# Two raw slots and three slots of split weights instead of four and two, with the split at the middle of a tile

## What is computed

```python
for i in range(DEPTH):
    h = rmsnorm(x, norm_g[i])
    proj = jnp.einsum('bsd,dn->bsn', h, w_in[i])
    ...
    ya = forgetting_attention(qa, ka, va, logf) * jax.nn.silu(za)
    yb = nsa_attention(qb, qb_rot, k_cmp, v_cmp, k_sel, vsb, k_win, vwb, gates) * jax.nn.silu(zb)
    yc = differential_attention(qc, kc, vc, lam, lam_init, diff_subln_g[i]) * jax.nn.silu(zc)
    g = jax.nn.sigmoid(mg).reshape(B, S, N_BRANCH, D)
    merged = g[:, :, 0] * (ya @ w_br_a[i]) + g[:, :, 1] * (yb @ w_br_b[i]) + g[:, :, 2] * (yc @ w_br_c[i])
    x = x + merged @ w_out[i]
    x = x + jax.nn.sigmoid(x @ w_ple_gate[i]) * (p[i] @ w_ple[i])
return rmsnorm(x, final_g)
```

## Time and profile before

| | us |
| --- | --- |
| median of 3 runs | 1508.64 |
| lowest, highest | 1507.59, 1510.21 |
| the profiled execution's own time | 1507.86 |
| its span in the profile | 1506.0 |
| PE busy | 1476.4 |
| DVE busy | 939.5 |
| ACT busy | 635.4 |

### The profile page before, as it was taken

One profiled execution on the slowest core, in us unless ns is written; L12 is line 12 of the kernel. 1 busy time (PEld: TensorE's weight loads), 2 busy tenths in 40 slices (PEclk: granted clock), 3 DMA queues, 4 the chain that ended last, 5 costly groups with the idle time before them and its releaser, 6 DMA issues.

```text
span 1506.0 us, 22241 instructions
## 1 busy us (share of the span) xinstructions
PE 1476.4 (98%) x7765; PEld 1225.9 (81%) x7765; DVE 939.5 (62%) x2197; ACT 635.4 (42%) x1499; POOL 75.4 (5%) x79
## 2 busy tenths in 40 slices
PE   8999999999999999999999999999999999999997
PEld 6778888888888887887787887888888888878885
DVE  6866765655656676454576668655555666755544
ACT  6543434444444444343444434344344444434343
POOL 1000000000001000000100000000000010000011
PEclk9999999999999999999999999999999999999998
DMA  7324443324325553332332335423343354433232
GB/s 196 90 78 119 112 113 78 73 75 107 77 69 134 140 129 87 100 101 70 109 104 77 106 100 135 109 58 76 80 100 81 99 129 124 112 99 109 80 88 74
DMA packets 259262, 150.48 MB, mean 100 GB/s; under 512 B 47482, under 2 KB 247764, under 8 KB 259156
## 3 DMA queue, kind: packets, MB, share of 16 engines
q1 hardware_dynamic: 259156, 149.11, 37.9%
HBM read 118.67 MB, written 2.10 MB: 80 GB/s over the span
## 4 chain that ended last, share of the span: by engine, by line
PE 79%; DVE 8%; DMA 4%; ACT 3%; SPq 2%; issue 2%; POOL 1%; ACTq 0%; DVEq 0%
PE D L774 21%; PE D L776 20%; PE D L775 19%; PE Ob L965 7%; PE T L943 4%; DMA arena<-rcs 3%; DVE w_lo L1329 2%; PE S L930 2%; PE S L931 2%; SPq L593 1%; ACT w_hi L1095 1%; PE S L920 1%; DMA rcs<-rx 1%; SPq L675 1%; ACT probs L1207 1%
## 5 line engine op out<-in xcount | busy, mean ns | idle before, releaser
L774 PE MATMUL D<-h_hi,w_hi 128*128 128x512 f32 x1264 | 537.9, 426 | 2.7 <-DVE w_lo L1329 1.7
L776 PE MATMUL D<-h_lo,w_hi 128*128 128x512 f32 x1264 | 496.1, 392 | 0.0
L775 PE MATMUL D<-h_hi,w_lo 128*128 128x512 f32 x1264 | 494.3, 391 | 0.0
L1329 DVE TENSOR_TENSOR w_lo<-raw,w_hi 128x512 fp32r<-128x512 f32 (+2 forms) x504 | 292.9, 621 | 256.3 <-ACT w_hi L1095 255.2
L1095 ACT ACTIVATE w_hi<-raw 128x512 fp32r<-128x512 f32 (+2 forms) x504 | 263.5, 569 | 245.8 <-PE D L776 243.5
L1207 ACT ACTIVATE probs<-probs,nmax 128x128 f32<-128x128 f32 (+3 forms) x256 | 142.0, 555 | 331.6 <-DVE nmax L1580 331.5
L776 PEld LDWEIGHTS D<-h_lo,w_hi 128*128 128x128 f32 x1264 | 237.2, 188 | 53.1
L774 PEld LDWEIGHTS D<-h_hi,w_hi 128*128 128x128 f32 x1264 | 238.8, 189 | 45.7 <-issue 6.3
L775 PEld LDWEIGHTS D<-h_hi,w_lo 128*128 128x128 f32 x1264 | 239.3, 189 | 30.3 <-issue 0.5
L1580 DVE CUSTOM_DVE_ANT_0 probs<-S,maskb 128x128 f32<-128x128 f32 (+3 forms) x256 | 115.1, 487 | 25.0 <-PE S L931 12.3
L556 DVE COPY pT<-T 128x128 f32<-128x128 f32 (+3 forms) x160 | 77.6, 487 | 59.5 <-PE T L943 59.0
(11 more groups left out here) (249 smaller groups left out, 1602.4 us busy)
## 6 DMA issues: line engine op xcount, KB each, us to landing
raw<-in_w_in_dram SPq DMA_DIRECT2D x124, 512.0 KB, 3.9
arena<-rcs SPq DMA_DIRECT2D x48, 256.0 KB, 4.4
raw<-in_w_in_dram SPq DMA_DIRECT2D x32, 256.0 KB, 3.7
arena<-rcs SPq DMA_DIRECT2D x64, 128.0 KB, 2.3
raw<-in_w_out_dram SPq DMA_DIRECT2D x16, 512.0 KB, 4.0
raw<-in_w_ple_gate_dram SPq DMA_DIRECT2D x16, 512.0 KB, 4.1
rcs<-rx SPq DMA_DIRECT2D x80, 64.0 KB, 2.0
raw<-in_cmp_w_k_dram SPq DMA_DIRECT2D x8, 512.0 KB, 3.7
```

The costliest lines, as they stand in the source:

```text
L774: pe.matmul(o, w_hi[:, sl, cs], hi[:, k, :], start=(k == 0), stop=False)
L775: pe.matmul(o, w_lo[:, sl, cs], hi[:, k, :], start=False, stop=False)
L776: ins = pe.matmul(o, w_hi[:, sl, cs], lo[:, k, :], start=False, stop=last)
L1329: TT(w_lo[:, sl, half], raw[:, ring(L, t, RAW), half], f(w_hi[:, sl, half]), ALU.subtract).then_inc(M["dve_lo"], 1)
```

## The change

`raw` gets two slots instead of four and the split weights three instead of two; the memory of both together stays the same. `weight_halves` goes: ACT and DVE split both halves of tile t + 2 when they come to the step in the middle of tile t. SP loads tile t + 4 instead of t + 6 at the end of tile t, and at a layer's start two tiles ahead of the small loads, two behind them. The loops are written out, since the slot of a tile (modulo 3) isn't the same in both turns; in them ACT and DVE ask for the split of tile t + 2 at the same place as before. In the gate phase both halves come ahead of the wait for the gate.

```diff
-RAW = 4
-SPL = 2
+RAW = 2
+SPL = 3
...
-def weight_halves(tiles, t):
-
-    nxt = tiles[t + 1][0] if t + 1 < len(tiles) else None
-    if nxt in ("w1k", "w1v"):
-        return ((), (0, 1)) if tiles[t][0] == "za" else ((0,), (1,))
-    if nxt and kt(nxt) == 8 and tiles[t][0] not in ("kcb", "vcb"):
-        return (), (0, 1)
-    return (0, 1), ()
...
-                    for t in range(RAW, 6):
+                    for t in range(RAW, 4):
                         static_load(t)
...
-                        if it[0] == "end" and it[1] + 6 < T0 + 4:
-                            static_load(it[1] + 6)
+                        if it[0] == "end" and it[1] + 4 < T0 + RAW:
+                            static_load(it[1] + 4)
...
-                    with pe.Fori(0, NM // 2 - 2) as i:
+                    for i in range(NM // 2 - 2):
...
-                                dense(kind, t, k)
+                                dense(kind, t + 4 * i, k)
...
                     for it in items:
                         what = it[0]
+                        if what == "mm" and it[2] == steps(tiles[it[1]][0]) // 2:
+                            hi(it[1] + 2)
...
                             D = Dn[ring(L, t, 2)]
-                            ahead, behind = weight_halves(tiles, t)
-                            if ahead:
-                                hi(t + 2, parts=ahead)
...
-                            if behind:
-                                hi(t + 2, parts=behind)
...
                         t = T2 + 2 * m
-                        weights_ahead(t, (0,))
+                        weights_ahead(t, (0, 1))
                         act.wait_ge(M["pe_dense"], t + 1)
                         act.wait_ge(M["dve_evac"], DE2 + m - 1)
                         A(th[:, m % 2, :], Dn[ring(L, t, 2)][:], ACT.Tanh, scale=0.5).then_inc(M["act_evac"], 1)
-                        weights_ahead(t, (1,))
                         weights_ahead(t + 1, (0, 1))
...
                         elif what == "mm":
                             t, k = it[1:]
+                            if k == steps(tiles[t][0]) // 2:
+                                lo(t + 2)
                             if (t, k) == (0, NM - 1):
                                 norm_chain()
...
-                            ahead, behind = weight_halves(tiles, t)
-                            lo(t + 2, parts=ahead)
...
-                            lo(t + 2, parts=behind)
```

More of the change, by code:

```diff
@@ L1023, in _ @@
                         ins.then_inc(M["pe_p"], 1)
-                    with pe.Fori(0, NM // 4) as i:
+                    for i in range(NM // 4):
                         for j in range(4):
@@ L1033, in _ @@
                                     pe.wait_ge(M["dve_merge"], k + 1)
-                                dense("out", t, k)
+                                dense("out", t + 4 * i, k)
                     def xg_transpose(m):
@@ L1080, in _, with hi @@
                     M, raw_ld, last_layer = MM[L], raw_lds[L], L == DEPTH - 1
[L1081 to L1092, removed]
+                    def hi(t, parts=(0, 1)):
+                        sl, n = ring(L, t, SPL), kt(kind_of(t)) * P
+                        act.wait_ge(raw_ld[t % RAW], landed_at(t))
+                        if t >= SPL:
+                            act.wait_ge(M["pe_dense"], t - SPL + 1)
+                        elif L:
+                            act.wait_ge(MM[L - 1]["pe_dense"], slot_user(t, SPL) + 1)
                         for h in parts:
@@ L1237, in _ @@
                     hi(T0 + 3)
-                    with act.Fori(0, NM // 2 - 2) as i:
+                    for i in range(NM // 2 - 2):
                         for j in range(4):
                             t = T0 + 2 + j
-                            hi(t + 2, i)
+                            hi(t + 2 + 4 * i)
                             if j % 2 == 0:
@@ L1261, in _ @@
                         A(y_hi[:, c, :], b[:], ACT.Copy).then_inc(M["act_p"], 1)
-                    with act.Fori(0, NM // 4) as i:
+                    for i in range(NM // 4):
                         for j in range(4):
                             t = T1 + j
-                            hi(t + 2, i)
+                            hi(t + 2 + 4 * i)
                             act.wait_ge(M["dve_evac"], i * 4 + (DE1 + j + 1))
@@ L1322, in _, with lo @@
                     TT, STT, TS, RED = dve.tensor_tensor, dve.scalar_tensor_tensor, dve.tensor_scalar, dve.tensor_reduce
-                    def lo(t, i=None, k=8, parts=(0, 1)):
-                        sl, n = ring(L, t, SPL), (kt(kind_of(t)) if i is None else k) * P
+                    def lo(t, parts=(0, 1)):
+                        sl, n = ring(L, t, SPL), kt(kind_of(t)) * P
                         for h in parts:
                             half = slice(h * n // 2, (h + 1) * n // 2)
-                            dve.wait_ge(M["act_hi"], 2 * t + 1 + h if i is None else i * 8 + (2 * t + 1 + h))
+                            dve.wait_ge(M["act_hi"], 2 * t + 1 + h)
                             TT(w_lo[:, sl, half], raw[:, ring(L, t, RAW), half], f(w_hi[:, sl, half]), ALU.subtract).then_inc(M["dve_lo"], 1)
@@ L1677, in _ @@
                         TT(acc[:, n, :], acc[:, n, :], rt[:], ALU.add).then_inc(M["dve_acc"], 1)
-                    with dve.Fori(0, NM // 2 - 2) as i:
+                    for i in range(NM // 2 - 2):
                         for j in range(4):
                             t = T0 + 2 + j
-                            lo(t + 2, i)
+                            lo(t + 2 + 4 * i)
                             if j % 2:
@@ L1712, in _ @@
                         TT(y_lo[:, c, :], b[:], f(y_hi[:, c, :]), ALU.subtract).then_inc(M["dve_p"], 1)
-                    with dve.Fori(0, NM // 4) as i:
+                    for i in range(NM // 4):
                         for j in range(4):
```

## The result

The changed kernel takes 1527.78 us (median of four runs, 1526.98 to 1528.33) against 1509.22 us of the kernel before beside it: a ratio of 1.0124, 95% interval 1.0112 to 1.0137. It is slower by 18.6 us, where the forecast was 7.4 us and the range ended at 1524. The profiled execution has a span of 1525.8 us, 19.8 more than before.

The account below looks back on a forecast made before the run. TensorE, busy 1476.4 of 1506.0 us, was taken as the bound. Losses of 18.0 us less gains of 10.6 gave net +7.4, so 1515.3 profiled and 1516 as the median; range 1509 to 1524.

Parts of the forecast that it names:

- own signs of being wrong: PE's layer-start wait under 2 us, keys' low half not delayed, or new waits over 0.5 us in stages 4 to 7.
- The forecast's own case: Whole kernel: losses of 18.0 us less gains of 10.6, net +7.4, 1516 us; chance 0.42.
- The clock falls: Rival, start of layer 1: PE's hold of some 5 us lowers the clock, 3 us more, 1519; chance 0.27.
- Loss 4: Stages 8 to 10: splits between high and low halves delay queries' and keys' low halves; 5.7 us, bounds 0 to 9.
- Loss 1: Start of layer 1: tile 2's late load and its split hold up the norm chain and PE; 4.8 us, bounds 3 to 6.
- Loss 2: Start of layer 0: ScalarE's copies for tile 2 precede tile 0's evacuation, delaying PE; 0.9 us, bounds 0 to 1.2.
- Loss 3: Stage 3: tile 31's late load delays PE 2.9 us, 5.8 in both layers; a hold before tile 19, 0.8 in both.
- The gains: Waits removed: gate phases 3.6 us, stage 0 1.7, stages 0 to 3 2.8, unit 11 2.0, stages 4 to 7 0.5; 10.6 together.
- Two slots are enough: Rival, stages 3 and 8 to 10: loads land before ScalarE asks, so 4 us faster, 1504.6; chance 0.09.
- Holds everywhere: Rival: some thirty late loads per layer each show on PE by 0.15 us, 8 us more, 1524; chance 0.13.
- It comes out even: Rival: the losses of stages 3 and 8 to 10 come at half, about +1.5 us, 1510; chance 0.09.

Follow-up runs that it names:

- e9: Kernel before, loops written out, plus four planted TensorE holds in the output projection (6, 7, 8 and 10 VectorE sums): 1541.91 us.
- e10: Kernel before, loops written out, plus four planted TensorE holds in the output projection (4, 5, 5 and 4 VectorE sums): 1521.13 us.
- e15: Kernel before, loops written out, plus four planted TensorE holds in the output projection (5 VectorE sums each): 1524.42 us, one run.
- e2: Changed kernel, with the weights of the kc tiles and the brb tile behind zc split one step later in stages 8 to 10: 1513.0 us.
- e1: Changed kernel, with layer 1's load of tile 2 back ahead of the wait for the layer's end and the eight small loads: 1519.35 us.
- e13: Changed kernel, with layer 1's weights of tile 2 split behind the norm chain and their load left late: 1518.89 us.
- e12: Kernel before, loops written out, with two raw slots and loads two tiles later, splits at their old places: 1507.96 us.
- e7: Changed kernel with the edits of e1 and e2, and the load at each tile's end issued ahead of the swap: 1499.98 us.
- e11: Changed kernel, with splits back at the places of the kernel before and loads issued ahead of the swaps: 1513.87 us.

## Why the prediction was wrong

The direction and the places were right; the size was not, 18.6 us for 7.4. Of the prediction's own signs of being wrong none came: PE's wait at the layer's start was 5.6 us, the keys' low half was later, and no new wait of over 0.5 us stands in stages 4 to 7. Two steps failed.

**The clock had no term in the sum.** The forecast's own case left it out; the rival *The clock falls* had it, but only in the start of layer 1, at 3 us, and gave 1519. Losses 3 and 4 were forecast as holds too, the largest of 2.9 us, and the step that failed is that I asked of the longest hold alone whether it would bring the clock down. The changed kernel fell in five places: tiles 32 and 76 in two layers, 6.4 us by their shifts, and 2.7 of the 8.18 at the start of layer 1 (PE's 5.80 us from 773.20 on ran at a mean of 0.54, so 5.3 us at the lower level), 9.1 us in all. e9, e10 and e15 show that a hold alone does this. The Trainium skill's statement (TensorE: Matmul & The Clock Gate, Loop structure matters more than you think) that waits between matmuls can leave the engine at the lower clock is what the trace shows, at five places and not one; it had been right to take it as a rival and wrong to give it one place.

**Loss 4 was mis-sized**: 5.7 us forecast, 10.3 measured without the clock (2.86 + 2.97 in layer 0, 2.85 + 0.45 + 1.15 in layer 1). The delay of one low half was right, 0.66 us for the 0.7 to 1.3 said. What was missing is that I took queries and keys each by itself, while the keys' swap waits for the queries' put, so that they add, and that a later put may also take longer to land: 2.8 us at the keys' put in layer 1, for the 1.25 of the sum. e2 shows the order as the cause. In layer 0 the last part of the keys' put for unit 10 also took 6.5 us from issue to landing (510.96 to 517.44), 4.8 in layer 1. Two weight loads were issued behind it at 512.21 and 514.87, and the DMA engines were busy 0.95 of the time from 514.5 to 517.5; but layer 1 has two such loads as well, so what made the difference stays open.

**Loss 1** was right: 4.8 forecast, 8.18 less 2.7 of clock measured, 5.5. The start of layer 1 in the changed kernel (it answers to the earlier trace rows):

```profile
764.01 1.06 SPq L614 DMA_DIRECT2D raw<-in_w_in_dram  x2
...
768.47 1.15 ACT L1081 ACTIVATE w_hi<-raw 128x512 fp32r<-128x512 f32 x2 [7.22 <-DMA raw<-in_w_in_dram]
769.13 1.29 DVE L1311 TENSOR_TENSOR w_lo<-raw,w_hi 128x512 fp32r<-128x512 f32 x2 [5.32 <-ACT w_hi L1081]
...
770.34 0.16 DVE L1348 TENSOR_SCALAR nrm<-T 128x4 f32<-128x4 f32 x1
...
773.17 2.08 PE L834 MATMUL T<-rcs,ones 128*128 128x512 f32 x2 [5.61 <-DVE rcs L1354]
```

The load is issued behind the small ones, ScalarE waits for it, VectorE for ScalarE, the norm chain stands behind both, and PE behind the chain, where 2.08 us for two matmuls (1.12) shows the clock at once. e1 and e13 add that it takes both, the late load and the split ahead of the chain: mending either takes the hold and its clock away, with 0.2 us left in e1 and 1.2 in e13.

**Loss 2** was 0.9 and is 0.86. **Loss 3** was 5.8 for tile 31 and is 4.2 (2.21 + 1.98), 0.8 for tile 19 and none there, but 0.95 at tile 27. The path was the one described: the load of tile 31 kept ScalarE at its copy to 194.99 and VectorE to 195.65, maxima and exponentials behind them, tanh, zs at 199.70:

```profile
190.51 6.83 SPq L614 DMA_DIRECT2D raw<-in_w_in_dram  x4
...
194.99 1.15 ACT L1081 ACTIVATE w_hi<-raw 128x512 fp32r<-128x512 f32 x2 [4.51 <-DMA raw<-in_w_in_dram]
...
199.70 0.69 DVE L1461 SCALAR_TENSOR_TENSOR zs<-th,D 128x512 f32<-128x512 f32 x1 [0.92 <-ACT th L1144]
...
200.53 0.47 PE L764 MATMUL D<-h_hi,w_hi 128*128 128x512 f32 x1 [2.89 <-DVE zs L1461]
```

**The gains** were 10.6 and are about 12.2; the gate phase of layer 0 gave 3.1 of it, seven times 0.40 and once 0.31. (The 248 matmuls in 55.00 us of the earlier trace rows make 0.22 us each, not 0.23; the 0.40 came out all the same.)

**The rivals.** *Two slots are enough* failed by its own test: the load of tile 31 was not there by 192. But as a statement on the slots alone it holds: e12 shows that two raw slots cost nothing where the split stands at the end of a tile, and there the Trainium skill's double buffering (Trainium Kernel Development and Optimization, Best Practices) agrees with the runs (1507.96 us against 1508.2). *Holds everywhere* found no support: outside the named places the tiles of stages 4 to 7 shift by 0.5 us at most. *It comes out even* was wrong with the forecast. In sum: losses without the clock 23.2 for 18.0, clock 9.1 for none, gains 12.2 for 10.6; 20.1 us on the span for 7.4.

## What to carry to other kernels

A work item that is asked for earlier in an in-order queue must be ready earlier, or all that is listed behind it pays. Here the third split slot was worth 11 to 14 us and halving the raw slots cost nothing; putting the splits in the middle of tiles cost 30.6, nearly all of it at three kinds of place. The splits left at the ends of tiles give a kernel 0.75% below the one before; the middle of tiles with three splits put elsewhere comes within what the runs can tell of it. The same order of loads was good with one order of splits (e7) and bad with the other (e11), because a load waits for its slot and holds up what is behind it. When a forecast contains several holds of an engine whose clock can fall, price the clock behind each of them, and follow a delay through a chain whose next link waits for the last.

## What the runs showed of the hardware

- A hold of TensorE of 4.0 us or more brought the granted clock down to 0.5 each time; one of 2.9 us did so in three of six planted cases and one of 1.8 us in neither of two; of those not planted, one of 1.6 us (e7) and two of three of 2.1 us (e11) did. The stretches at 0.5 lasted 3.4 us, 6.8 with some holds (4.0 and 6.3 us among them) and 10.2 with the one of 8.5; the hold of 5.2 us had 3.4. Length of hold and length of stretch don't go strictly together.
- Behind a short hold the clock can fall late: behind that of 197.6 to 200.5 in the changed kernel PE worked at full clock until 201.7, so the price stands in other instructions than the wait, in the tile behind it. In the holds of 4.0 us and more it fell before PE was back, by 0.2 us (5.2 us) to 4.3 (8.5 us), and that part of the low stretch cost nothing.
- The mean granted clock of the whole span hides this: 20.5 us at 0.5 in 1526 change it by 0.7%.
